# A hybrid attention and retention layer on 8 cores: the prefix's last key norm behind the next q projection, and the last chunks' output work in another order

## The reference

```python
h = rmsnorm(x, norm_g)                                   # x: (4, 8192, 1024)
aq, ak, av, az, rq, rk, rv, rz = split(h @ w_in)         # 512,128,128,512,256,256,512,512
a = sliding_window_attention(aq, ak, av, sinks) * silu(az)
r = retention(rq, rk, rv, ret_gn_g) * silu(rz)           # state * decay + k^T v, chunk by chunk
x = x + concat([a, r]) @ w_out
out = rmsnorm(x, final_g)
```

## Time and profile before

| | |
|---|---|
| median of 3 runs | 685.19 us (684.84 to 688.24) |
| the profiled execution | 683.99 us |
| its slowest core's span | 682.5 us (cores: 676.8 to 682.5) |
| TensorE busy | 605.0 us (89%), granted clock 0.973 |
| VectorE, ScalarE, GpSimd busy | 539.5 us (79%), 410.2 us (60%), 193.0 us (28%) |
| DMA | 94 MB, mean 138 GB/s |

### The profile page before, as it was taken

How to read it: one execution, slowest core, us unless ns; L and a number is a source line. 1 busy time by engine, 2 the same in 40 slices (tenths; PEclk the granted TensorE clock), 3 DMA queues, 4 the chain that set the end, 5 groups by cost and what they waited for, 6 DMA issues and landing times.

```text
span 682.5 us, 19190 instructions; the slowest of 8 cores (676.8 to 682.5 us)
## 1 busy us (share of the span) xinstructions
PE 605.0 (89%) x5059; PEld 369.4 (54%) x5059; DVE 539.5 (79%) x1178; ACT 410.2 (60%) x730; POOL 193.0 (28%) x251
## 2 busy tenths in 40 slices
PE   0586787888999989999999999999999999998964
PEld 0464565545565555555555665555555665555531
DVE  0788877455788878888888988898889888887865
ACT  3688767665475555566556566666566655655532
POOL 2644342002122232222232223232221323332221
PEclk9999989798999989999999999999999999998978
DMA  7999998532343534565246434444374444432213
GB/s 193 339 317 339 329 292 259 178 77 64 79 79 96 107 81 133 121 115 142 63 110 157 110 110 110 110 109 110 109 117 128 121 127 91 122 76 76 69 47 108
DMA packets 89338, 94.15 MB, mean 138 GB/s; under 512 B 68624, under 2 KB 69008, under 8 KB 89232
## 3 DMA queue, kind: packets, MB, share of 16 engines
q1 hardware_dynamic: 89232, 92.93, 49.8%
HBM read 59.88 MB, written 16.78 MB: 112 GB/s over the span
## 4 chain that ended last, share of the span: by engine, by line
PE 75%; DMA 7%; DVE 6%; issue 5%; ACT 3%; POOL 2%; SPq 1%; DVEq 0%; POOLq 0%; ACTq 0%
PE ps L702 36%; PE ps L1015 14%; PE ps L708 11%; DMA wstage<-w_r 4%; PE ps L865 4%; PE ps L898 2%; DMA dkt<-dk_pre 2%; DMA wstage<-w_o 1%; PE ps L942 1%; PE ps L984 1%; PE ps L988 1%; PE ps L884 1%; PE ps L752 1%; PE ps L923 1%; DVE Sst L931 1%
## 5 line engine op out<-in xcount | busy, mean ns | idle before, releaser
L702 PE MATMUL ps<-Wa,hT 128*128 128x512 bf16 (+2 forms) x1032 | 166.5, 315 | 4.4 <-ACT hT L509 2.7
L702 PEld LDWEIGHTS ps<-Wa,hT 128*128 128x128 bf16 x1032 | 88.5, 99 | 61.1 <-issue 5.0
L1015 PE MATMUL ps<-Wo,mixT 128*128 128x512 bf16 x512 | 116.2, 380 | 1.1 <-DMA mixT<-mix 1.1
L702 PE MATMUL ps<-Wb,hT 128*128 128x512 bf16 x512 | 115.7, 379 | 0.1
L677 POOL TENSOR_TENSOR stat<-stat,neghalf 128x1 f32<-128x1 f32 x64 | 38.4, 623 | 232.0 <-DVE stat L674 183.5
L874 POOL TENSOR_SCALAR_AFFINE_SELECT PT<-PT 128x1024 bf16<-128x1024 bf16 x63 | 75.1, 1201 | 58.7 <-ACT PT L868 56.8
L1015 PEld LDWEIGHTS ps<-Wo,mixT 128*128 128x128 bf16 x512 | 50.3, 98 | 55.9 <-issue 2.4
L702 PEld LDWEIGHTS ps<-Wb,hT 128*128 128x128 bf16 x512 | 48.8, 98 | 53.3 <-issue 0.3
L825 ACT ACTIVATE gate<-ps 128x512 f32<-128x512 f32 x64 | 38.2, 597 | 56.9 <-PE ps L702 16.4
L671 ACT ACTIVATE junk<-xs 128x1024 bf16<-128x1024 f32 x64 | 67.2, 1050 | 7.0 <-DMA xs<-x_all 4.2
L868 ACT ACTIVATE PT<-ps,negC 128x1024 bf16<-128x1024 f32 x64 | 70.9, 1116 | 0.4 <-PE ps L865 0.2
(11 more groups left out here) (121 smaller groups left out, 1012.9 us busy)
## 6 DMA issues: line engine op xcount, KB each, us to landing
xs<-x_all SPq DMA_DIRECT2D x64, 512.0 KB, 8.5
out<-yy SPq DMA_DIRECT2D x32, 512.0 KB, 3.5
wstage<-w_r SPq DMA_DIRECT2D x16, 640.0 KB, 11.3
tb<-tabs SPq DMA_DIRECT2D x32, 256.0 KB, 4.8
wstage<-w_o SPq DMA_DIRECT2D x8, 512.0 KB, 7.4
wstage<-w_k SPq DMA_DIRECT2D x2, 512.0 KB, 6.9
gate<-cs_pre SPq DMA_DIRECT2D x2, 512.0 KB, 13.1
fg_rep_s<-fg_rep SPq DMA_DIRECT2D x1, 512.0 KB, 10.3
```

What stands on the lines that cost most here:

```text
L702: S.add("pe", lambda e, kb=kb: e.matmul(bank[:, c0:c0 + n], lhsT=hT[c % 2][:, kb * 128:(kb + 1) * 128], rhs=W[:, kb, w0:w0 + n], start=(kb ...
L1015: S.add("pe", lambda e, kb=kb, bank=bank, half=half: e.matmul(bank[:, 0:512], lhsT=mixT[s2][:, kb * 128:(kb + 1) * 128], rhs=Wo[:, kb, hal ...
```

## The change

- norm_k of chunk 31 is no longer a part of that chunk's projection. It is issued in chunk 32's, behind the q projection and its copies.
- The state update (KV) of chunk 63 is left out; nothing reads it.
- In the last rounds of the loop store and O are taken out of their places. At t = 63, behind scT of 63, stand store(60), O(61), store(61). At t = 64, behind PV and OR of 63, stand O(62), M(63), store(62), O(63), store(63). M(62) stays where the table has it, at the beginning of t = 64.
- M of chunk 63 is done by TensorE (8 transposes into a bank, and a copy by VectorE) instead of by DMA.
- The final scaling of chunk 63 and its store are done in two halves of 512 columns, each with a buffer of its own for the waits (b_yl) and a semaphore (sl0, sl1).

```diff
@@ -795,7 +796,6 @@
             mm_tok(bank, bb, 128, Wa, b_Wa, A_AV, 128, c)
             ev_kv(c, bank, bb)
             ev_sqk(c, bank, bb)
-            norm_k(c)
 
     def st_P_main(c, part):
         s2 = c % 2
@@ -806,6 +806,10 @@
             S.add(cp(aqT[s2][:], bank[:, 0:512]), reads=[bb], writes=[b_aqT[s2]])
             S.add("act", lambda e, bank=bank: e.activation(out=sqq[0][:], in_=bank[:, 0:512], func=AF.Square),
                   reads=[bb], writes=[b_sqq[0]])
+            if c == NP:
+                S.cur_chunk = c - 1
+                norm_k(c - 1)
+                S.cur_chunk = c
             bank, bb = alloc("A")
             mm_feat(bank, bb, 0, Wa, b_Wa, A_AK, c)
             mm_tok(bank, bb, 128, Wa, b_Wa, A_AV, 128, c)
@@ -916,6 +920,8 @@
             reads=bb + [b_gate[s2]], writes=[b_mix[s2]])
 
     def st_KV(c):
+        if c == NT - 1:
+            return
         sn = (c + 1) % 2
         bank, bb = alloc("B")
         rvv = rv[c % 3][:].rearrange("p (r j e) -> p j r e", r=2, j=2)
@@ -1005,6 +1011,16 @@
 
     def st_M(c):
         s2 = c % 2
+        if c == NT - 1:
+            bank, bb = alloc("A")
+            pb = bank.bitcast(BF16)
+            for half in range(2):
+                for kb in range(half * 4, half * 4 + 4):
+                    S.add("pe", lambda e, kb=kb: e.transpose(pb[:, kb * 128:(kb + 1) * 128],
+                                                             mix[s2][:, kb * 128:(kb + 1) * 128], ident_bf[:]),
+                          reads=[b_mix[s2], b_const], writes=[bb])
+            S.add(cp(mixT[s2][:], pb[:, 0:1024], ("dve",)), reads=[bb], writes=[b_mixT[s2]])
+            return
         dma_tr(mixT[s2][:], mix[s2][:], b_mixT[s2], b_mix[s2], f"tm{s2}")
 
     def st_O(c):
@@ -1028,12 +1044,24 @@
               reads=[b_stat2[s2]], writes=[b_stat2[s2]])
         S.add("pool", lambda e: e.tensor_tensor(out=st[:, 2:3], in0=st[:, 1:2], in1=neghalf[:, 0:1], op=ALU.pow),
               reads=[b_stat2[s2], b_misc], writes=[b_stat2[s2]])
+        if c == NT - 1:
+            for h in range(2):
+                hs = slice(h * 512, (h + 1) * 512)
+                S.add("dve", lambda e, hs=hs: e.scalar_tensor_tensor(out=yy[s2][:, hs], in0=yy[s2][:, hs], scalar=st[:, 2:3],
+                                                                     in1=fg_rep[:, hs], op0=ALU.mult, op1=ALU.mult),
+                      reads=[b_yy[s2], b_stat2[s2], b_constB], writes=[b_yl[h]])
+            return
         S.add("dve", lambda e: e.scalar_tensor_tensor(out=yy[s2][:], in0=yy[s2][:], scalar=st[:, 2:3], in1=fg_rep[:],
                                                       op0=ALU.mult, op1=ALU.mult),
               reads=[b_yy[s2], b_stat2[s2], b_constB], writes=[b_yy[s2]])
 
     def st_store(c):
         s2, m = c % 2, c - NP
+        if c == NT - 1:
+            for h in range(2):
+                hs = slice(h * 512, (h + 1) * 512)
+                S.add("sp", dma(out_d[m * CH:(m + 1) * CH, hs], yy[s2][:, hs]), reads=[b_yl[h]], dmaq=f"sl{h}")
+            return
         S.add("sp", dma(out_d[m * CH:(m + 1) * CH, :], yy[s2][:]), reads=[b_yy[s2]], dmaq=f"st{s2}")
 
     def run_stage(name, c):
@@ -1103,6 +1131,21 @@
         for task in w_tasks.get(t, ()):
             task()
         for name, off_pre, off in order:
+            if t >= NT - 1:
+                if name in ("O", "store") and t > NT - 1:
+                    continue
+                if name == "M" and t - off == NT - 1:
+                    continue
+                if name == "GT" and t == NT - 1:
+                    run_stage("store", NT - 4)
+                    run_stage("O", NT - 3)
+                    run_stage("store", NT - 3)
+                if name == "G" and t == NT:
+                    run_stage("O", NT - 2)
+                    run_stage("M", NT - 1)
+                    run_stage("store", NT - 2)
+                    run_stage("O", NT - 1)
+                    run_stage("store", NT - 1)
             if name == "G":
                 for c in range(max(0, t - 3), NP):
                     if t == min(c + 3, NP):
```

More of the change, by code:

```diff
@@ L467, in build_program @@
     b_Gbf, b_GT = b_yy
+    b_yl = [Buf("yyl0"), Buf("yyl1")]
     stat2, b_stat2 = slots("stat2", 2, [128, 4], F32)
@@ L487, in alloc_pair @@
         return ps_all[:, i * 512:(i + 2) * 512], [b_bank[i], b_bank[i + 1]]
-    qnames = ["pe", "act", "dve", "pool", "const", "constB", "cs0", "cs1", "dkt", "th0", "th1", "tm0", "tm1"]
+    qnames = ["pe", "act", "dve", "pool", "const", "constB", "cs0", "cs1", "dkt", "th0", "th1", "tm0", "tm1", "sl0", "sl1"]
     qnames += [f"ws{i}" for i in range(NST)]
@@ L1119, in build_program @@
     S.finalize()
-    S.emit(nc, block, sems, [f"st{i}" for i in range(2)])
+    S.emit(nc, block, sems, ["st0", "st1", "sl0", "sl1"])
     es.close()
```

## The result

The changed kernel takes **701.15 us** (median of 4 executions) beside 685.37 us for the kernel before (4): a ratio of 1.021, with a 95% interval of 1.016 to 1.026. One of the four executions of the changed kernel was disturbed (781 us), and the ratio goes by the other three, whose median is 699.68 us. Forecast were 692.5 us, which is 1.010, and a range of 684 to 699. The direction was right, the size was half of what came, and the time lies above the range (by 0.7 us even without the disturbed execution).

A forecast was written before the change was run, and what follows sets the result against it. TensorE was taken to bound the kernel, with three quarters of the chain of waits. Transition -5.0, loop +6.3 and end +6.0 gave +7.3 us on the profiled 683.99; with the median 1.2 above, 692.5 us, range 684 to 699.

The forecast's parts named there:

- the loop's term: Rounds 36 to 63: the planner's reshuffled order on VectorE, ScalarE and GpSimd adds waits at the score matmuls, +6.3 us.
- the baseline: Loop of the kernel before: 14.7 us lost without falls of the clock, read from core 7.
- the last three rounds: Rounds 60 to 62: yy additions between mix and gg delay the scores; losses of 1.9, 1.3 and 2.9 us.
- The end: After norm_q of 63: mix 62's transposition waits behind store(61) on SP's queue, delaying the last projection; +6.0 us.
- the transition: Chunk 31 to round 36: moving norm_k behind the q projection removes TensorE's wait for the squared keys; -5.0 us.
- the +6.5 worked out: The end's chain, before allowing for the omitted last state update and halved store, which made it +6.0 us.
- the cast: Transition: a Wo cast with a column, moved from ScalarE to GpSimd ahead of the stat powers, taken at 2.8 us.
- a measured twin: Loop: a round of the kernel before with a like VectorE order, whose measured loss was taken for the new round.
- Rival 1: The reshuffled loop costs nothing, new patterns hidden and old ones staying: 686.2 us; chance 0.18.
- rival 2: VectorE's additions to Sst come in time in nearly all rounds, loop -6: 680.2 us; chance 0.12.
- rival 3: The norm_k move brings -2 instead of -5, as TensorE waits for hT and sqk anyway: 695.5 us; chance 0.08.
- Rival 4: The clock falls at most of the new waits, loop +11 and end +8: 699 us; chance 0.10.

The follow-up runs named there:

- e8: e3 with the casts of Wo with a column kept on ScalarE, not GpSimd; 0.994 of the kernel before, median 682.5 us.
- e7: e3 plus chunk 63's state update left out, its mix transposed by TensorE, scaling and store halved, without the reordering; 0.993 of the kernel before, 681.3 us.
- e3: Kernel before with the norm_k move alone, instructions issued from t = 34 on bound to the old engines and order; 0.991, 681.0 us.
- e5: The whole change, with instructions issued from t = 34 to 62 bound to the engines and order of the kernel before; 1.004, 689.1 us.
- e6: Kernel before with the norm_k move, planner free but giving instructions that free the four B banks 2 us of lead; 1.042, 715.7 us.

## Why the prediction had the direction and half the size

The step that failed is the loop's term: +6.3 us stood in the sum and +10.3 was measured, as the baseline was read from a core whose clock falls and the last three rounds were costed too low. Two smaller terms add to it. The end was +6.0 for +7.9, and the transition -5.0 for -3.7, where GpSimd's hold on VectorE had been put at nothing. All three missed to the same side.

**The end** (+6.0 forecast, +7.9 measured, bounds +3.5 to +8). The mechanism was the one named, and each step came in its order. Counted from norm_q of 63, forecast and measured on core 3: last score matmul 14.4 and 14.4; O(61) done 21.4 and 22.1; final scaling of 61 done 25.7 and 26.6; mixT 62 landed 29.6 and 31.1; O(63) starts 36.2 and 37.7; from its last matmul to the end 7.2 and 7.1. The wait was forecast as 7 us and is 8.1. On this core the chain was 1.5 us longer than worked out. 0.7 is output projection 61, taken at 4.8 us and measured at 5.46, with a granted clock of 0.66 from 663.3 to 668.8; 0.2 stands between it and the scaling's end. The other 0.6 stands between the scaling of 61 and the landing: 3.9 us forecast, 4.5 measured, since the transposition is issued 1.24 us after the store ahead of it, where 0.5 had been taken. The rest of the miss is the step from the +6.5 worked out to the +6.0 taken.

**The transition** (-5.0 forecast, -3.7 measured). norm_q of chunk 32 is 4.7 us earlier, the q projection of 33 5.1 on core 3 (4.9 forecast). The key projection starts at 121.8, forecast 122.1, so the move itself brought what it was to bring. What was left out stands behind: round 32 is 16.1 us instead of 15.2. A third of that is core 4 alone (18.0 us, with its q projection at 3.54 us instead of 1.95). For the rest e8 points to GpSimd's product, which stops VectorE: without it the round is 15.3. That this hold alone makes the round longer is not shown, as e8 gives ScalarE the casts at the same time, and e7, with the product, has as short a transition as e8 (77.4 and 77.6). The forecast costed the cast by its own length (2.8 us taken, 1.89 measured) and saw only who waits for GpSimd, not whom GpSimd holds.

**The loop** (+6.3 forecast, +10.3 measured). That much of the cost would lie in rounds that the diff does not touch was right, and e3 and e5 show it. Two steps carry the miss, and the clock adds a third part:

- The baseline. "14.7 us without falls of the clock" was core 7, taken for a core whose clock never falls as its row says 1.00 over 440 us. It does fall there, in round 61. Core 7, kernel before, a stretch of that round and the whole round, then core 4 over the loop (the number behind POOL is the granted clock):

```profile
611.00:616.00 5.00, 3.09 (x27) 2.92 (x28) 3.23 (x9) 2.81 (x6) 1.09 (x2) 0.67 0.01 3
601.11:620.78 19.67, 17.46 (x138) 10.88 (x137) 15.43 (x34) 10.31 (x19) 5.97 (x7) 0.91 0.21 55
...
201.12:640.31 439.19, 427.36 (x3619) 255.44 (x3672) 379.95 (x840) 268.45 (x506) 124.85 (x134) 1.00 0.42 109
```

  Core 4, with no such round (its round 61 takes 18.15 us, with the same wait of 2.21), has 439.2 us, so 13.1 without falls. The prediction's reading of round 61, 4.0 us lost where the clock falls, so holds 2.4 of waiting and 1.6 of clock. The changed kernel's core 6 has 448.2, so 22.1, where the sum of the rounds had given 20.6. The order's part is +9.0, not +5.9: 1.6 from the baseline, 1.5 from the rounds.
- The rounds (loss over 15.78 us, forecast and core 6 measured): 40: 2.2 and 2.4; 43: 1.9 and 2.2; 44, 49 and 50 together: 4.2 and 4.1; 41 and 42: 1.8 and 1.0; 53: 1.0 and 0.6; 58 and 59: 1.6 and 0.9; 60: 1.9 and 2.9; 61: 1.3 and 2.5; 62: 2.9 and 3.0. Where a round had a measured twin the forecast held to 0.4 us a round; the three worked out without one, 60 to 62, were 2.3 us short together. In round 60 TensorE waits for the Exp, mix and gg (0.8, 0.7 and 0.6 us), in round 61 for sqk as well as for the second addition (1.0 and 1.1); the forecast had looked at what stands ahead of gg and of the second addition alone.
- Falls of the clock: they add 2.8 us on the mean core (in round 40 on cores 3 and 5, in 43 on the five others beside core 6, and in 62 on all but core 6) where before has 1.5. Forecast were 0.4 more than before, measured 1.3 more.

Rival 1 (the loop costs nothing) and rival 2 (faster) are out by the changed kernel itself, rival 3 (the move brings 2) by the transition. Rival 4 put the loop at +11 and the end at +8, and so has both sizes nearly right, but by luck: its mechanism, a fall of the clock at most of the new waits, is not what the rounds show, as falls are 1.3 of the loop's 10.3 us. The range of 684 to 699 was too narrow since it left little room for two large terms at once: the loop at its +10 and the end at its +8 were each inside their bounds (0 to +13, +3.5 to +8) and came together. Their sum with the transition is -3.7 + 10.3 + 7.9 = +14.5, and the rest of +16.0 is the prefix of this execution.

## What to carry to other kernels

Where a greedy planner orders the engines, an edit at one place is an edit of every round behind it: compare the order round by round, and test the edit with the old order held fast before judging it. The order itself was worth more than the edit (9 us for one good round repeated, against 4 for the move), and e6 shows that an order has to serve both bank pools, not the one where the waits stand. On a queue that works in order, ask of each DMA that is moved up what it waits for, since all behind it waits for that as well.

## What the runs showed of the hardware

- VectorE's addition of two 128x256 tiles in SBUF takes 0.43 us alone, and 1.93 and 2.09 us while GpSimd multiplies 1024 columns (1.98 and 1.89 us): both times it starts behind GpSimd's instruction and ends 0.3 us behind it. SBUF — State Buffer (the Trainium skill, section Who interferes with whom) says that a VectorE instruction with two inputs in SBUF contends with a GpSimd instruction that reads SBUF, and that the port pair which the two share is an exclusive lock; the trace agrees. This rule was not weighed in the prediction, and spoke against the planner's move of two casts.
- GpSimd's product of 1024 float32 columns with one column took 1.89 and 1.98 us. GPSIMD Engine Reference (the Trainium skill, section 3.1 Elementwise) has 4497 ns for a float32 addition of 2048 columns; half of it, an estimate of 2.25 us for 1024, is 0.3 to 0.4 too long for this product.
- In the end of the changed kernel a store of 512 KB landed 2.7 us after its issue and one of 256 KB 2.1 us: a half lands 0.6 us sooner.

```profile
out<-yy SPq DMA_DIRECT2D x2, 512.0 KB, 2.7
out<-yy SPq DMA_DIRECT2D x2, 256.0 KB, 2.1
```

- After the same waits (1.5 and 0.5 us in round 40, 1.3 and 0.5 in round 43), the granted clock falls on some cores and not on others, in the same kernel and execution: round 40 takes 19.7 us on core 3 and 18.1 on core 0, round 43 18.0 and 19.6. Seven of the eight cores have one such fall in these two rounds, of 1.6 us each, and core 6 has none.
